# Opening of a two-block transformer kernel: modulation vectors and tokens taken tile by tile, gates and the first four weight jobs multiplied side by side

## The chip, the cores and the metric

The kernel runs on one core of one Trainium2 chip. The metric is the device time of one execution in microseconds (us). Three runs of the kernel before gave 2936.73 (the median), 2933.33 and 2941.17 us.

## What is computed

The reference is a stack of two blocks on 512 tokens of width 1024. Only the start of the first layer matters here: a modulation vector is computed from the condition `c`, the tokens are scaled and shifted by it, and the result `u` is multiplied by the input projection of an mLSTM mixer, whose columns are q, k, v, o and eight gate columns.

```
cs = jax.nn.silu(c)
for i in range(DEPTH):
    ada = cs @ w_ada[i] + b_ada[i]
    sh1, sc1, g1, sh2, sc2, g2 = [t[:, None, :] for t in jnp.split(ada, 6, axis=-1)]
    u = x * (1.0 + sc1) + sh1
    y = _mlstm_mixer(u, m_w_in[j], ...)        # even layers
# in _mlstm_mixer
proj = u @ w_in
qk, v, o, gates = jnp.split(proj, [s1, s2, s3], axis=-1)
qk = jax.nn.silu(_causal_dwconv(qk, conv_w, conv_b))
ig, lf = gates[..., :H], jax.nn.log_sigmoid(gates[..., H:])
```

All the rest (mixers, layer norms, FFNs, the second network) follows and is not touched.

## The kernel before, in words

Data is held transposed: features on the 128 partitions, tokens along the free side. `XT` is the stream in 8 tiles (KT = 8) of 128 features x 512 tokens. A weight matrix is cut into jobs of 128 output columns; a job is 128 x 8 x 128 numbers, 512 KB. There are 392 jobs (`wst`), numbered j in the order of the phases: `qk` (jobs 0 to 15), `v` (16 to 23), `gate_o` (24 to 31), `res` and so on.

Each job goes through the same line. SP loads it into one of two `RAW` slots (`load_raw`, L467; it waits for `lo_done` to reach j-1, so that the slot is free). ACT rounds it into `WH`, one of four slots (`round_hi`, L790, or `round_next`, L859; it waits for `pe_job` to reach j-3). POOL subtracts to get the low part `WL` (`lo`, L552). PE multiplies three times for each of 8 tiles: WH with the high part `U1h` of the input, WH with its low part `U1l`, WL with `U1h`, which is 24 matmuls of 128 x 512 (L1507). In `qk` DVE then applies a four-tap convolution (L1711, L1713) and ACT a SiLU (L949). In `v` ACT copies the result out (L953), PE turns it by four transposes (L1428), and DVE copies it into `VX` (L1809). The banks of `qk` and `v` are 0, 1, 4 and 7.

The modulation vectors are computed on DVE: a tile of `ast` (128 rows x 1024, 512 KB) is multiplied with `CB`, the SiLU of the condition, and summed along the row (`ada_sum`, L1637); four sums are then added to their bias and written to `MOD` (`ada_out`, L1649).

The opening of the kernel before has these steps:

- SP issues, in one queue: CB, 16 tiles of `ast` with their first slots in `ADA0` (8 slots), between them `PRM` (parameters), `GW` (gate weights), the whole `XT` behind tile 7, and the first two jobs behind tiles 10 and 12; then four constants, then the jobs from 2 on.
- DVE sums the 16 tiles, and only then writes `G2` = 1 + scale (L1686) and `B2` = shift (L1687) for all 8 tiles.
- ACT makes `U1h` and the full-precision copy `UF` tile by tile (L872, L873); DVE subtracts to get `U1l` (L1675).
- PE multiplies the gate weights with each tile as it comes (L1417, 24 matmuls into bank 2), and then jobs 0, 1, 2, ... one after the other.
- DVE works out the gate rows behind that (from L1693 to L1706), with an exponential and a logarithm from ACT (L878, L879). PE transposes the rows at the start of `v` (L1572).

Every engine executes its own instructions strictly in the order in which they are written; the order across engines is kept by semaphores.

Of the kernel before, what the change touches and what calls it, by code (L numbers as in the profile page):

```python
# [21 lines left out]
F32 = mybir.dt.float32  # L22
# [183 lines left out]
def build(nc, a, out):  # L206
    with ExitStack() as stack:
# [253 lines left out]
        def _(sp):  # L461
# [28 lines left out]
            for n, p in enumerate(phases):  # L490
                def body(i, p=p, ada_before=None):
                    for u in range(4):
                        if not (p["j0"] == 0 and is_first(i) and u < 2):
                            load_raw(i * 4 + (p["j0"] + u), u % 2)
# [288 lines left out]
        def _(act):  # L783
# [65 lines left out]
            def round_next(i, p, u):  # L849

                c = p["j0"] + u + 3
                if isinstance(i, int):
                    j = 4 * i + c
                    if j < njobs:
                        round_hi(j, j % 4)
                    return
# [20 lines left out]
            act.wait_ge(S("gate_abs"), 1)  # L877
            steps.link(act.activation(GR[0:4, 2], GR[0:4, 1], ACT.Exp))  # L878
            act.activation(GR[0:4, 3], GR[0:4, 2], ACT.Ln, bias=1.0).then_inc(S("gate_ln"), 1)  # L879
# [150 lines left out]
            for n, p in enumerate(phases):  # L1030
# [25 lines left out]
                if first(p, "v", 0):  # L1056
                    act.wait_ge(S("silu_done"), 16)
                if first(p, "res", 0):
# [352 lines left out]
        def _(pe):  # L1411

            pe.wait_ge(S("gate_lo"), 1)
            for k in range(KT):
                pe.wait_ge(S("u_ready"), k + 1)
                for m, (w, x) in enumerate(((GWh, U1h), (GWh, U1l), (GWl, U1h))):
                    mm = pe.matmul(BANK[2][:], w[:, k], x[:, k, 0:T], start=k == 0 and m == 0, stop=k == KT - 1 and m == 2)  # L1417
            mm.then_inc(S("gates_pe"), 1)
# [146 lines left out]
            for n, p in enumerate(phases):  # L1565
                if first(p, "v", 0):
                    pe.wait_ge(S("const_land"), 16 * 4)

# [21 lines left out]
                if first(p, "res", 1):  # L1590
# [26 lines left out]
        def _(dve):  # L1617
# [54 lines left out]
            def u_lo():  # L1672
                for t in range(KT):
                    dve.wait_ge(S("uf_done"), t + 1)
                    dve.tensor_tensor(U1l[:, t], UF[:, t, 0:T], U1h[:, t].bitcast(F32), ALU.subtract).then_inc(S("u_ready"), 1)  # L1675

            dve.wait_ge(S("prm_land"), 16)
            dve.wait_ge(S("cb_ready"), 1)
            for g in range(4):
                for u in range(4):  # L1680
                    j = 4 * g + u
                    dve.wait_ge(S(f"ada_begin{j % 8}"), 16 * (j // 8 + 1))
                    ada_sum(g, 0, u, ADA0[:, j % 8])
                ada_out(g, 0)
            dve.wait_ge(S("ada_evac"), 4)
            link(dve.tensor_scalar(G2[:, :, 0:1], mod(0, 1), 1.0, None, ALU.add))  # L1686
            dve.tensor_copy(B2[:, :, 0:1], mod(0, 0)).then_inc(S("g2_done"), 1)  # L1687
            u_lo()


            dve.wait_ge(S("gates_pe"), 1)
            gb = COL["gate_b"][0]
            link(dve.tensor_scalar(GR[0:4, 0], BANK[2][0:4, :], PRM[0:4, gb:gb + 1], None, ALU.add))  # L1693
            link(dve.tensor_scalar(GR[0:4, 5], BANK[2][32:36, :], PRM[32:36, gb:gb + 1], None, ALU.add))
            dve.scalar_tensor_tensor(out=GR[0:4, 1], in0=GR[0:4, 5], scalar=-1.0, in1=GR[0:4, 5], op0=ALU.mult, op1=ALU.min)\
                .then_inc(S("gate_abs"), 1)
            link(dve.tensor_scalar(GR[0:4, 4], GR[0:4, 5], 0.0, None, ALU.min))
            dve.wait_ge(S("gate_ln"), 1)
            link(dve.tensor_tensor(GR[0:4, 6], GR[0:4, 4], GR[0:4, 3], ALU.subtract))

            link(dve.tensor_tensor_scan(GR[0:4, 7], GR[0:4, 6], GR[0:4, 6], 0.0, ALU.add, ALU.bypass))
            link(dve.tensor_tensor(GM[0:4, 1], GR[0:4, 0], GR[0:4, 7], ALU.subtract))
            link(dve.tensor_tensor_scan(GM[0:4, 0], GM[0:4, 1], GM[0:4, 1], 0.0, ALU.max, ALU.bypass))
            dve.tensor_tensor(GM[0:4, 2], GR[0:4, 7], GM[0:4, 0], ALU.add).then_inc(S("gate_rows"), 1)
            dve.wait_ge(S("gate_rows"), 1)
            link(dve.memset(VX[:, :, :, DK:DK + 2], 1.0))  # L1706
# [498 lines left out]
            for n, p in enumerate(phases):  # L2205
# [5 lines left out]
                if first(p, "v", 0):  # L2211
                    dve.wait_ge(S("gate_cols_pe"), 1)
                    dve.tensor_copy(COLS[:], BANK[2][:, 0:32]).then_inc(S("gate_cols"), 1)
# [205 lines left out]
```

## Time and profile before

| | |
|---|---|
| median of the three runs | 2936.73 us |
| the profiled execution | 2937.88 us |
| its span, first to last instruction | 2936.1 us |
| granted TensorE clock, mean | 0.979 |
| PE busy | 2797.1 us, 95% of the span |
| DVE, POOL, ACT busy | 1593.2, 1093.2, 1046.6 us |
| moved from HBM | 324.50 MB, 111 GB/s over the span |

The page has, besides, the span in 40 slices of 73.4 us, the chain of work that ended last, and groups of instructions. A row of the timeline reads: start, time taken, engine, line, operation, output<-inputs, and in brackets how long its engine was idle before it and what ended that. PE is TensorE's matmuls, PEld its weight loads, SPq the queue of SyncE.

### The profile page before, as it was taken

How to read it: one execution, taken by the hardware profiler on the slowest of the kernel's cores; microseconds unless marked ns; L12 is line 12 of the kernel's file. 1: busy time of each engine (PE TensorE's matmuls, PEld its weight loads, DVE VectorE, ACT ScalarE, POOL GpSimd, SP SyncE). 2: the span in 40 equal slices, each digit the busy share in tenths (PEclk: the TensorE clock that was granted, in tenths of full speed). 3: DMA queues.
4: the chain of work that ended last, by engine and by line, in shares of the span. 5: the costliest groups of instructions: out<-in, count | busy, mean ns of one | idle time of the engine just before them, and what ended most of it. 6: DMA issues, size and time to landing. Idle time of an engine off the chain costs nothing.

```text
span 2936.1 us, 37960 instructions
## 1 busy us (share of the span) xinstructions
PE 2797.1 (95%) x13936; PEld 2391.5 (81%) x13936; DVE 1593.2 (54%) x2341; ACT 1046.6 (36%) x1689; POOL 1093.2 (37%) x510
## 2 busy tenths in 40 slices
PE   4998899999899899999999999999999999999998
PEld 3885788887776678887897999999997977778887
DVE  6536766966555669986522423755553487332111
ACT  3333353423465443324311232222223338443222
POOL 2440254444422254445531333323335233334443
PEclk9999899999999899999899999999999999999999
DMA  5351345553321145554111122333332122122232
GB/s 214 112 186 44 108 139 197 186 189 126 131 84 61 51 141 193 188 186 136 44 61 56 50 87 79 129 129 129 116 128 79 58 90 66 62 86 93 97 97 86
DMA packets 89955, 329.83 MB, mean 112 GB/s; under 512 B 9956, under 2 KB 10724, under 8 KB 89320
## 3 DMA queue, kind: packets, MB, share of 16 engines
q1 hardware_dynamic: 85392, 312.21, 30.6%
q10 hardware_dynamic: 4440, 16.00, 1.6%
q8 instruction: 75, 1.23, 0.2%
q14 instruction: 48, 0.39, 0.0%
HBM read 324.50 MB, written 2.10 MB: 111 GB/s over the span
## 4 chain that ended last, share of the span: by engine, by line
PE 58%; DVE 2%; POOL 1%; ACT 1%; issue 1%; DVEq 0%; ACTq 0%; POOLq 0%
PE pair L1505 26%; PE pair L1507 18%; PE bank L1507 4%; PE pair L1347 1%; PE bank L1300 1%; PE pair L1363 1%; PE bank L1380 1%; PE bank L1347 1%; PE bank L1437 0%; PE pair L1461 0%; PE pair L1320 0%; PE bank L1320 0%; POOL UF L534 0%; PE bank L1287 0%; POOL UF L538 0%
## 5 line engine op out<-in xcount | busy, mean ns | idle before, releaser
L552 POOL TENSOR_TENSOR WL<-RAW,WH 128x1024 fp32r<-128x1024 f32 x392 | 983.4, 2510 | 1679.0 <-ACT WH L859 1065.3
L859 ACT ACTIVATE WH<-RAW 128x1024 fp32r<-128x1024 f32 x276 | 290.3, 1052 | 351.3 <-PE pair L1505 181.5
L1637 DVE CUSTOM_DVE_ANT_0 ADA<-ADA,CB 128x1024 f32<-128x1024 f32 x128 | 237.7, 1863 | 117.2 <-DMA ADA<-in_ast 105.9
L1770 DVE SCALAR_TENSOR_TENSOR XT<-pair,GATE,XT 128x512 f32 (+1 forms) x96 | 72.0, 750 | 348.0 <-PE pair L1507 179.7
L1505 PE MATMUL pair<-Uh,WH 128*128 128x384 f32 x832 | 214.0, 338 | 2.1 <-issue 2.1
L1505 PE MATMUL pair<-Ul,WH 128*128 128x384 f32 x832 | 211.1, 334 | 0.0
L1505 PE MATMUL pair<-Uh,WL 128*128 128x384 f32 x832 | 211.1, 334 | 0.0
L1507 PE MATMUL bank<-U1h,WH 128*128 128x512 f32 x480 | 187.2, 390 | 0.0
L1507 PE MATMUL bank<-U1h,WL 128*128 128x512 f32 x480 | 186.8, 389 | 0.0
L1507 PE MATMUL bank<-U1l,WH 128*128 128x512 f32 x480 | 186.8, 389 | 0.0
L1507 PE MATMUL pair<-U1h,WH 128*128 128x512 f32 x448 | 175.5, 392 | 2.8 <-POOL WL L552 2.8
L1507 PE MATMUL pair<-Hh,WH 128*128 128x512 f32 x432 | 169.2, 392 | 8.1 <-DVE Hl L644 8.1
L1507 PE MATMUL pair<-U1h,WL 128*128 128x512 f32 x448 | 175.1, 391 | 0.0
L1507 PE MATMUL pair<-U1l,WH 128*128 128x512 f32 x448 | 174.9, 390 | 0.0
L1507 PE MATMUL pair<-Hl,WH 128*128 128x512 f32 x432 | 168.2, 389 | 0.0
L1507 PE MATMUL pair<-Hh,WL 128*128 128x512 f32 x432 | 168.1, 389 | 0.0
L790 ACT ACTIVATE WH<-RAW 128x1024 fp32r<-128x1024 f32 x116 | 122.1, 1053 | 105.9 <-DMA RAW<-in_wst 51.9
L1505 PEld LDWEIGHTS pair<-Uh,WH 128*128 128x128 f32 x832 | 150.3, 188 | 6.1 <-issue 6.0
L1505 PEld LDWEIGHTS pair<-Ul,WH 128*128 128x128 f32 x832 | 150.3, 188 | 0.0
L1505 PEld LDWEIGHTS pair<-Uh,WL 128*128 128x128 f32 x832 | 150.2, 188 | 0.0
L1826 DVE SCALAR_TENSOR_TENSOR TT<-pair,TT 128x512 f32<-128x512 f32 x64 | 44.3, 692 | 192.1 <-ACT TT L982 102.8
L1505 PE MATMUL pair<-Hh,WL 128*128 128x384 f32 x512 | 129.9, 334 | 0.0
(416 smaller groups left out, 6170.7 us busy)
## 6 DMA issues: line engine op xcount, KB each, us to landing
RAW<-in_wst SPq DMA_DIRECT2D x392, 512.0 KB, 3.5
ADA<-in_ast SPq DMA_DIRECT2D x192, 512.0 KB, 4.5
NB<-in_nbias ACTq DMA_DIRECT2D x8, 768.0 KB, 4.2
XT<-in_xt SPq DMA_DIRECT2D x1, 2048.0 KB, 15.4
STRIP<-in_strip ACTq DMA_DIRECT2D x8, 256.0 KB, 2.7
CB<-in_cb ACTq DMA_DIRECT2D x4, 512.0 KB, 4.1
DX<-in_dx ACTq DMA_DIRECT2D x1, 2048.0 KB, 8.0
out_xt<-XT SPq DMA_DIRECT2D x1, 2048.0 KB, 6.2
```

The source lines that it names most:

```text
L552: pool.tensor_tensor(WL[:, s4], RAW[:, s2], WH[:, s4].bitcast(F32), ALU.subtract)\
L790: act.activation(WH[:, u], RAW[:, u % 2], ACT.Copy).then_inc(S("hi_done"), 1)
L859: act.activation(WH[:, c % 4], RAW[:, c % 2], ACT.Copy).then_inc(S("hi_done"), 1)
L1300: mm = pe.matmul(BANK[bank][:, 0:w], FG[:, tok0 + i_, t, q * P:(q + 1) * P], mats[:, q, i_], start=i_ == 0 and q == 0, stop=i_ == tiles - ...
L1347: mm = pe.matmul(BANK[b][:], x[:, k, tok], flat(w[:, i, 4 * kk:4 * kk + 4]), start=k == 0 and m == 0, stop=k == KT - 1 and m == 2)
L1363: mm = pe.transpose(BANK[2 + c][:, s * P:(s + 1) * P], ZP[:, i % 3, c, s * P:(s + 1) * P], IDENT[:])
L1380: mm = pe.matmul(BANK[4][64 * c:64 * c + 64, b * P:(b + 1) * P], VN[:, tile, (2 * t + c) * NHD:(2 * t + c + 1) * NHD], PTN[:, i % 2, c, s ...
L1505: mm = pe.matmul(dst, w[:, u, k], x[:, k, c:c + HALF_TC], start=st and m == 0, stop=en and m == 2)
L1507: mm = pe.matmul(bank_of(p, u)[:], w[:, u, k], x[:, k, 0:T], start=st and m == 0, stop=en and m == 2)
L1637: dve.tensor_tensor_reduce(tile, tile, cb[:, 0], 1.0, 0.0, ALU.mult, ALU.add, AD[:, u, 0:1])\
L1770: ins = dve.scalar_tensor_tensor(out=flat(XT[:, ds(jl, 1)]), in0=bank[:], scalar=gate_of(jl), in1=flat(XT[:, ds(jl, 1)]), op0=ALU.mult, op ...
L1826: ins = dve.scalar_tensor_tensor(out=TT[:, u % 2, 0:T], in0=bank[:], scalar=0.0, in1=TT[:, u % 2, 0:T], op0=ALU.max, op1=ALU.mult)
```

## The change

- SP's order is by feature tile. For each k of 0 to 7 it loads the two `ast` tiles that this feature tile needs (row tile k, the shift, and row tile 8 + k, the scale) and then the 256 KB of `XT[:, k]`. Behind tile 0 come PRM, GW and jobs 0 and 1; behind tile 2 comes job 2, behind tile 3 job 3, each with its wait for `lo_done`. The wait of `XT[:, k]` is folded into the semaphore of the second `ast` tile.
- DVE, per k: two sums, the subtraction for tile k - 1 (`opening_lo`), and then `B2` and `G2` of tile k alone, which read the sums and the bias directly.
- ACT makes `U1h` and `UF` of tile t as soon as `g2_done` reaches t + 1. It rounds job 2 behind tile 2, job 3 behind tile 3, and jobs 4 and 5 behind tile 7. `round_next` then leaves out the jobs that have been rounded, and rounds job 6 between the first and second SiLU.
- PE (`opening`), per k: jobs 0 and 1 with tile k, the gates with tile k, and, from k = 2 on, jobs 2 and 3 with tile k - 2; the last two tiles of jobs 2 and 3 come at the end. Job 2's and job 3's first matmuls wait for `lo_done` of 3 and 4. These are the same 120 matmuls as before. The loop over `qk` then starts with job 4.
- The gate rows (DVE and ACT) move from behind the opening to the start of `v`, and their transposes on PE and the copy on DVE from the start of `v` to the start of `gate_o`.

```
-            for j in range(16):
-                at_least(sp, S("ada_done"), j - 7)
-                sp.dma_start(ADA0[:, j % 8], a["ast"][j]).then_inc(S(f"ada_begin{j % 8}"), 16)
-                if j == 1:
-                    sp.dma_start(PRM[:], a["prm"]).then_inc(S("prm_land"), 16)
-                if j == 3:
-                    sp.dma_start(GW[:], a["gw"]).then_inc(S("gw_land"), 16)
-                if j == 7:
-                    sp.dma_start(XT[:], a["xt"]).then_inc(S("x_land"), 16)
-                if j in (10, 12):
-                    load_raw(j // 2 - 5, j // 2 - 5)
+            for k in range(KT):
+                for n, j in ((2 * k, k), (2 * k + 1, KT + k)):
+                    at_least(sp, S("ada_done"), n - 7)
+                    sp.dma_start(ADA0[:, n % 8], a["ast"][j]).then_inc(S(f"ada_begin{n % 8}"), 16)
+                sp.dma_start(XT[:, k], a["xt"][:, k]).then_inc(S(f"ada_begin{(2 * k + 1) % 8}"), 16)
+                if k == 0:
+                    sp.dma_start(PRM[:], a["prm"]).then_inc(S("prm_land"), 16)
+                    sp.dma_start(GW[:], a["gw"]).then_inc(S("gw_land"), 16)
+                    load_raw(0, 0)
+                    load_raw(1, 1)
+                if k in (2, 3):
+                    load_raw(k, k % 2)
...
-            act.wait_ge(S("x_land"), 16)
-            act.wait_ge(S("g2_done"), 1)
             for t in range(KT):
+                act.wait_ge(S(f"ada_begin{(2 * t + 1) % 8}"), 32 * (t // 4 + 1))
+                act.wait_ge(S("g2_done"), t + 1)
                 act.activation(U1h[:, t], XT[:, t], ACT.Identity, ...)
                 act.activation(UF[:, t, 0:T], XT[:, t], ACT.Identity, ...)
-            round_hi(2, 2)
+                if t in (2, 3):
+                    round_hi(t, t)
+            round_hi(4, 0)
+            round_hi(5, 1)
...
+                for k in range(KT):
+                    pe.wait_ge(S("u_ready"), k + 1)
+                    for u in range(2):
+                        job(u, k)
+                    gates(k)
+                    if k >= 2:
+                        for u in range(2, 4):
+                            job(u, k - 2)
+                for u in range(2, 4):
+                    for k in range(KT - 2, KT):
+                        job(u, k)
...
+            for k in range(KT):
+                at_least(dve, S("g2_done"), k - 1)
+                for q in range(2):
+                    n = 2 * k + q
+                    dve.wait_ge(S(f"ada_begin{n % 8}"), (16 + 16 * q) * (n // 8 + 1))
+                    dve.tensor_tensor_reduce(ADA0[:, n % 8], ADA0[:, n % 8], CB[:, 0], 1.0, 0.0, ALU.mult, ALU.add,
+                                             AD[:, n % 4, 0:1]).then_inc(S("ada_done"), 1)
+                if k >= 1:
+                    opening_lo(k - 1)
+                dve.wait_ge(S("ada_done"), 2 * k + 2)
+                q = 2 * (k % 2)
+                dve.tensor_tensor(B2[:, k, 0:1], AD[:, q, 0:1], prm("bada", 2 * k), ALU.add)
+                dve.scalar_tensor_tensor(out=G2[:, k, 0:1], in0=AD[:, q + 1, 0:1], scalar=1.0, in1=prm("bada", 2 * (KT + k)),
+                                         op0=ALU.add, op1=ALU.add).then_inc(S("g2_done"), 1)
+            dve.wait_ge(S("g2_done"), KT)
+            dve.sem_inc(S("ada_evac"), 4)
+            opening_lo(KT - 1)
...
                 if first(p, "v", 0):
+                    gate_rows_dve()
+                if first(p, "gate_o", 0):
                     dve.wait_ge(S("gate_cols_pe"), 1)
```

## Rows read from the trace of the kernel before

**Rows 1.** The page: busy time, then two rows of its 40 slices.
```profile
PE 2797.1 (95%) x13936; PEld 2391.5 (81%) x13936; DVE 1593.2 (54%) x2341; ACT 1046.6 (36%) x1689; POOL 1093.2 (37%) x510
...
PE   4998899999899899999999999999999999999998
```
**Rows 2.** Timeline: PE at the opening, gates (L1417), then jobs 0 to 4 (L1507).
```profile
41.44 0.77 PE L1417 MATMUL pair<-U1h,GWh 128*128 128x512 f32 x1 [41.44 <-DVE U1l L1675]
42.01 0.63 PE L1417 MATMUL pair<-U1l,GWh 128*128 128x512 f32 x1
...
42.43 0.63 PE L1417 MATMUL pair<-U1h,GWl 128*128 128x512 f32 x1
...
47.42 0.40 PE L1417 MATMUL pair<-U1l,GWh 128*128 128x512 f32 x1
...
52.03 0.39 PE L1507 MATMUL pair<-U1h,WH 128*128 128x512 f32 x1
...
73.80 0.39 PE L1507 MATMUL pair<-U1h,WH 128*128 128x512 f32 x1
```
**Rows 3.** DMA issues in 0:80: count, size, median us to landing.
```profile
ADA<-in_ast SPq DMA_DIRECT2D x16, 512.0 KB, 11.9
...
PRM<-in_prm SPq DMA_DIRECT2D x1, 472.5 KB, 5.9
```
**Rows 4.** Timeline: the queue's first issue, then instructions that a landing released.
```profile
0.76 0.39 SPq L462 DMA_DIRECT2D CB<-in_cb  x1
...
4.33 1.06 ACT L862 ACTIVATE CB<-CB 128x1024 f32<-128x1024 f32 x1 [2.29 <-DMA CB<-in_cb]
...
8.03 1.23 DVE L1637 CUSTOM_DVE_ANT_0 ADA<-ADA,CB 128x1024 f32<-128x1024 f32 x1 [8.03 <-DMA PRM<-in_prm]
...
26.64 1.06 ACT L790 ACTIVATE WH<-RAW 128x1024 fp32r<-128x1024 f32 x1 [13.83 <-DMA RAW<-in_wst]
```
**Rows 5.** Timeline: POOL and DVE at 12, POOL at 144, DVE at 431.
```profile
12.89 2.34 POOL L556 TENSOR_TENSOR GWl<-GW,GWh 128x1024 fp32r<-128x1024 f32 x1 [12.42 <-ACT GWh L864]
13.04 3.26 DVE L1637 CUSTOM_DVE_ANT_0 ADA<-ADA,CB 128x1024 f32<-128x1024 f32 x1
...
144.90 5.74 POOL L552 TENSOR_TENSOR WL<-RAW,WH 128x1024 fp32r<-128x1024 f32 x2 [3.24 <-ACT WH L790]
...
431.00 2.36 DVE L1649 TENSOR_TENSOR MOD<-AD,PRM 128x4 f32<-128x4 f32 x1
```
**Rows 6.** Timeline: small DVE work, ACT's pair and DVE's subtraction for one tile.
```profile
38.78 0.17 DVE L1687 COPY B<-MOD 128x8 f32<-128x8 f32 x1
39.05 0.81 ACT L872 ACTIVATE U1h<-XT,B,G 128x512 fp32r<-128x512 f32 x1 [7.65 <-DVE B L1687]
39.77 0.80 ACT L873 ACTIVATE UF<-XT,B,G 128x512 f32<-128x512 f32 x1
...
40.60 0.69 DVE L1675 TENSOR_TENSOR U1l<-UF,U1h 128x512 fp32r<-128x512 f32 x1 [1.65 <-ACT UF L873]
```
**Rows 7.** Windows late in the kernel; columns end in granted clock, DMA share, GB/s.
```profile
2218.00:2222.00 4.00, 2.78 (x9) 2.13 (x9) 3.88 (x5) 1.67 (x3) 1.64 (x2) 0.50 0.00 0
```
**Rows 8.** Timeline of PE in that stretch.
```profile
2220.16 0.77 PE L1461 MATMUL pair<-Uh,WH 128*128 128x512 f32 x1 [1.22 <-ACT Uh L913]
...
2225.19 0.39 PE L1461 MATMUL pair<-Uh,WH 128*128 128x512 f32 x1
```
**Rows 9.** Timeline: gate rows now, first and last DVE step, and ACT's logarithm.
```profile
52.23 0.74 DVE L1693 TENSOR_SCALAR GR<-pair,PRM 4x512 f32<-4x512 f32 x1 [1.06 <-PE pair L1417]
...
56.44 0.63 ACT L879 ACTIVATE GR<-GR 4x512 f32<-4x512 f32 x1
...
63.87 0.09 DVE L1706 MEMSET VX<- 128x32 f32 x1
```
**Rows 10.** Timeline: the start of `v` on ACT and PE.
```profile
143.05 0.63 ACT L949 ACTIVATE QK<-TT 128x512 f32 x1 [3.85 <-DVE TT L1713]
...
150.78 0.60 PE L1428 MATMUL bank<-IDENT,TT 128*128 128x128 f32 x4
```

More of the change, by code:

```diff
@@ L492, in body @@
                     for u in range(4):
-                        if not (p["j0"] == 0 and is_first(i) and u < 2):
+                        if not (p["j0"] == 0 and is_first(i)):
                             load_raw(i * 4 + (p["j0"] + u), u % 2)
@@ L853, in round_next @@
                     j = 4 * i + c
+                    if c == u + 3 and i == 0:
+                        j = 6 if u == 1 else njobs
                     if j < njobs:
@@ L874, in _, with gate_rows_act @@
                     .then_inc(S("uf_done"), 1)
-            round_hi(2, 2)
-            act.wait_ge(S("gate_abs"), 1)
-            steps.link(act.activation(GR[0:4, 2], GR[0:4, 1], ACT.Exp))
-            act.activation(GR[0:4, 3], GR[0:4, 2], ACT.Ln, bias=1.0).then_inc(S("gate_ln"), 1)
+                if t in (2, 3):
+                    round_hi(t, t)
+            round_hi(4, 0)
+            round_hi(5, 1)
+            def gate_rows_act():
+                act.wait_ge(S("gate_abs"), 1)
+                steps.link(act.activation(GR[0:4, 2], GR[0:4, 1], ACT.Exp))
+                act.activation(GR[0:4, 3], GR[0:4, 2], ACT.Ln, bias=1.0).then_inc(S("gate_ln"), 1)
             def ln_act(p, idx):
@@ L1411, in _, with opening, gates, job @@
         def _(pe):
[L1413 to L1418, printed above, removed]
+            def opening():
+                def gates(k):
+                    if k == 0:
+                        pe.wait_ge(S("gate_lo"), 1)
+                    for m, (w, x) in enumerate(((GWh, U1h), (GWh, U1l), (GWl, U1h))):
+                        mm = pe.matmul(BANK[2][:], w[:, k], x[:, k, 0:T], start=k == 0 and m == 0, stop=k == KT - 1 and m == 2)
+                    if k == KT - 1:
+                        mm.then_inc(S("gates_pe"), 1)
+                def job(u, k):
+                    if k == 0:
+                        pe.wait_ge(S("lo_done"), u + 1)
+                    for m, (w, x) in enumerate(((WH, U1h), (WH, U1l), (WL, U1h))):
+                        mm = pe.matmul(bank_of(phases[0], u)[:], w[:, u, k], x[:, k], start=k == 0 and m == 0,
+                                       stop=k == KT - 1 and m == 2)
+                    if k == KT - 1:
+                        mm.then_inc(S("pe_job"), 1)
+                for k in range(KT):
[9 more added lines that the diff above has]
+                        job(u, k)
+            opening()
             def v_turn(i, p, u):
@@ L1589, in _ @@
                     neighbourhood_pe(pe)
-                if first(p, "res", 1):
+                if p["j0"] == 0:
+                    rounds(pe, p["n"] // 4 - 1, lambda i, p=p: stream(i + 1, p))
+                elif first(p, "res", 1):
                     stream(1, p)
@@ L1670, in rms_gains @@
                 link(dve.tensor_copy(B2[:, :, 0:n], mod(layer, vec, 0, n)))
[L1672 to L1675, printed above, removed]
             dve.wait_ge(S("prm_land"), 16)
             dve.wait_ge(S("cb_ready"), 1)
[L1679 to L1706, printed above, removed]
+            def opening_lo(t):
+                dve.wait_ge(S("uf_done"), t + 1)
+                dve.tensor_tensor(U1l[:, t], UF[:, t, 0:T], U1h[:, t].bitcast(F32), ALU.subtract).then_inc(S("u_ready"), 1)
@@ L2211, in _ @@
                 if first(p, "v", 0):
+                    gate_rows_dve()
+                if first(p, "gate_o", 0):
                     dve.wait_ge(S("gate_cols_pe"), 1)
```

17 lines of the change are left out of this document (added).

## Prediction

> **What bounds the kernel now.** I read the page first: PE is busy 95% of the span and near full in nearly every slice but the first [rows 1]. So a microsecond is won only where PE idles or is late, and the first slice is such a place. The timeline of PE there shows it idle until 41.44, then the gates, waiting for each tile, and jobs from 52.03 on, with nothing between them; job 4 starts at 73.80 [rows 2]. That instant is the whole measure of this change: from job 4 on the work is as before, so whatever job 4 gains, the end gains, unless a later stall takes it back. PE owes 120 matmuls before job 4 (24 for the gates, 96 for jobs 0 to 3). Their pitch is (73.80 - 52.03) / 96 = 0.227 us at full clock, 27.2 us in all, and 0.42 us in the first gates [rows 2]. So PE is given its tiles too late, and the question is when they can come.
>
> **The queue.** All bytes go through SP's one queue and land in order: CB (0.52 MB) is used at 4.33, PRM as the fourth transfer (2.06 MB in total) at 8.03, job 0 (9.92 MB) at 26.64 [rows 3, 4]. That is a rate of 0.42 MB/us, so a transfer is usable at 4.33 + (MB before its end - 0.52) / 0.42. The bytes don't change, only the order. By the new order: tile 0 at 7.5, PRM 8.6, GW 9.9, job 0 11.1, job 1 12.4, tile 1 15.5, tile 2 18.6, job 2 19.9, tile 3 23.0, job 3 24.2, then a tile each 3.1 us to tile 7 at 36.7. New: SP waits ahead of job 2 for the first `lo`, with the tiles 3 to 7 queued behind it. CB took 3.6 us from issue to use [rows 4], and the wait ends at 15.9 (below), so job 2 still comes by 19.9 and the wait costs nothing; its cover ends if `lo` is later than 16.3.
>
> **DVE and POOL.** This is what I think now sets the pace. A sum takes 1.22 us, but 3.26 when a POOL subtraction of 2.34 has begun just before; two POOL subtractions around a sum took 5.74 together; even a 128x4 addition took 2.36 once, where such small steps take 0.17 [rows 5, 6]. So an instruction with two inputs in SBUF and a POOL subtraction take turns, whole instruction by whole instruction. The Trainium skill says the same (SBUF — State Buffer, "Who interferes with whom": an exclusive lock), and the trace agrees by the 2.36 us row.
>
> Per tile DVE has two sums (2.3 us start to start), one subtraction (0.69) and two small ones (0.17 each) [rows 4, 6]: 3.35 us, slightly more than the 3.1 us of the queue. POOL's GWl and four `lo` add 5 turns of 2.4. Taking turns from 8.7: DVE sums tile 0 till 11.1; GWl 11.05 to 13.4; `lo` of job 0 till 15.9; of job 1 till 18.4, with B2 and G2 of tile 0 between. Sums and B2/G2 of tile 1 till 21.7, of tile 2 till 25.05. `U1l` of tile 0 is there at 21.4. ACT needs 1.5 us per tile [rows 6] and then rounds job 2 till 27.65; `lo` of job 2 gets its turn 28.1 to 30.5. G2 of tile 3 waits for it, is there at 30.8, ACT makes tile 3 till 32.4 and only then rounds job 3, till 33.4; its `lo` waits for two sums and a subtraction and ends at 36.25. From there DVE needs 3.35 us a tile: G2 of tile 7 at 46.65, the last `U1l` at 49.0 (38.78 and about 51 now).
>
> **PE.** It takes tiles 0, 1 and 2 between 21.4 and 30.8, then stands at job 3's first matmul until 36.3, because jobs 2 and 3 are taken up at k = 2. By then 30 of 120 matmuls are done. The other 90 take 20.4 us at 0.227, and each of their tiles is there in time. To this I add the clock. The first 13 gates ran at a pitch of 0.42, the lower of the two levels (1.2 GHz), and by 47.42 they had the upper one; late in the kernel, behind stops of PE, the granted clock is 0.50 and PE needs from 2220.16 to 2225.19 before a matmul of that shape takes 0.39 again [rows 2, 7, 8]. A stop of 5.5 us stands before the 90 matmuls, so I charge 13 of them the difference, 13 x 0.19 = 2.5. The bounds are 0 (the clock stays) and 5 (it comes back late). Job 4 thus starts at 36.3 + 20.4 + 2.5 = 59.2, and the gain is 73.8 - 59.2 = 14.6 us.
>
> A rule of the Trainium skill bears on this term: TensorE: Matmul & The Clock Gate, "What's actually happening", has the slow clock as the default and activity as what lifts it. By the rule the restart is slow and the sum is 14.6; if the stretch before the stop still counted, it would be 17.1. The rows at 2220 agree with the rule.
>
> **What goes elsewhere.** Job 4 must be rounded and subtracted between the end of job 0 and its start. Behind job 0's last matmul there are 24 others, 5.45 us; rounding and `lo` take 1.06 + 2.4 + 0.2 = 3.7. So 1.7 us are spare, and without them the price is what is missing. The four convolutions come in one burst on DVE and job 7 is rounded only behind them; it is not wanted before jobs 4 to 6 are through, 16 us: free.
>
> The gate rows at the start of `v` put a wait into ACT, with the rounding of job 19 and the copy of job 16 queued behind it, and fill DVE for 63.87 - 52.23 = 11.6 us, with its sum for the next vector and VX behind. Now the logarithm ends 4.85 us after DVE's first step [rows 9]. DVE is free at 142.9, just ahead of the last SiLU [rows 10]; so ACT is free at 147.8, rounds job 19 till 148.8 and copies job 16 till 149.4. PE's transposes of it come at 150.78 [rows 10], 1.4 us to spare; job 19 is wanted 6 us after them (24 matmuls and four transposes), also free. DVE, with two turns lost to POOL, reaches VX of job 16 at about 161; PE wants that two jobs behind 150.78, near 163. Both are close, so I charge 0, with 0 to 3 as bounds. The moved transposes and copy cost 0.7 wherever they stand. PE's, SP's and ACT's counts of instructions stay; DVE saves four small ones.
>
> **The sum.** Against the profiled execution: 2937.9 - 14.6 = 2923.3. The median of the runs is 1.15 below that execution, so 2922.2.
>
> **The rivals.** (A) One turn better: if G2 of tile 3 gets ahead of `lo` of job 2, all that follows is 2.2 us earlier, `lo` of job 3 ends at 34.05, and job 4 starts at 57.0, or at 54.5 if the clock also holds. The next bound is then the last `U1l`, 46.8 + 27 matmuls x 0.227 = 52.9. Gains of 17 to 19, 2917.5 to 2920. For it: turns hang on tenths of a microsecond. (B) Small waits add up: the 1.7 and 1.4 us of slack are used up, `v` stalls by 2 or 3 us, a `lo` comes one turn (2.4) later. Gain 5 to 10, 2927 to 2932. (C) No change: the clock stays low through the whole opening, as PE works in short bursts. 90 matmuls at 0.42 end at 74.1, so job 4 is no earlier and the time is 2937. The Trainium skill describes such a pattern (TensorE: Matmul & The Clock Gate, "HAM oscillation — how this bites in real kernels"). Against it: behind 36.3 PE has all its data and runs without a stop, as from 41.44, where the clock rose after 5.6 us [rows 2]. (D) Slower: the chain of turns is worse than I have it, so that job 4 comes behind 73.8. It needs SP held up: job 2, and behind it tile 3 and job 3, hang on `lo` of job 0. Were that at 31 instead of 15.9 (as now, where job 0 lands at 26.64), job 2 would land at 34.6 and job 3 at 39; with the 12 us that I have from job 3's landing to the end of its `lo` (24.2 to 36.25), and 22.9 of PE behind it, job 4 starts at 73.9. That is the point from which it decides; each us beyond costs one, and at 33 the time is 2939. Against it: 3.4 MB are ahead of the end of job 0 instead of 9.9. (E) The order doesn't matter since the bytes are the same: the last tile lands at 36.7, where by the same rate the last `ast` tile landed at 34.2 before (13.07 MB), and the tiles are ready at 49 instead of 51. True of the tiles, but the gain is in the 96 matmuls that lay behind them, so I give it nothing of its own.
>
> **How the numbers follow.** Forecast as summed, gains of 10 to 17: 0.55. A: 0.15. B: 0.20. C: 0.06. D: 0.04. The measurement tells about 0.3% of the kernel, 8.8 us, from no change. Faster by more than that: the forecast, A and a third of B, 0.76; within: the rest of B and C, 0.19; slower 0.05. The range is 2916 to 2931.5: it holds the forecast, A with both clock bounds and the scatter of a median of three runs below it, and most of B, and leaves out C, D and the worst of B.
>
> **What would show it.** PE's first matmul near 21.4 instead of 41.44; sums of 3.3 us where POOL works; a stop of PE for `lo` of job 3 until about 36; a pitch of 0.42 behind it for some 5 us; job 4 near 59; in `v` no idle PE ahead of the transposes. The forecast is wrong if PE waits for `u_ready` between tiles 3 and 7, if SP stands behind 16.3, or if the time saved by job 4 is not there at the start of `gate_o`.

## The result and the profile after

The changed kernel took 2918.53 us (median of 4 runs, 2916.05 to 2919.61) beside 2937.74 us for the kernel before (4 runs): a ratio of 0.9939, 95% interval 0.9927 to 0.9951. That is 19.2 us faster, where 14.6 us were forecast. Measured twice more (below) the gain was 15.5 and 13.9 us.

| | after |
|---|---|
| the profiled execution, its span | 2918.07, 2916.3 us |
| granted TensorE clock, mean | 0.977 |
| PE busy | 2795.3 us, 96% of the span |

The page shows the gain in one digit, that of the first slice, which was 4 [rows 1]. The work of PE is the same 13936 matmuls.

```profile
PE 2795.3 (96%) x13936; PEld 2390.7 (82%) x13936; DVE 1601.9 (55%) x2351; ACT 1045.7 (36%) x1688; POOL 1097.7 (38%) x510
...
PE   6998899999999899999999999999999999999998
```

The timeline of PE at the opening of the changed kernel, against [rows 2]: start, time taken, engine, line, operation.

```profile
21.81 0.79 PE L1436 MATMUL pair<-U1h,WH 128*128 128x512 f32 x1 [21.81 <-DVE U1l L1714]
22.40 0.63 PE L1436 MATMUL pair<-U1l,WH 128*128 128x512 f32 x1
...
31.27 0.39 PE L1436 MATMUL bank<-U1h,WL 128*128 128x512 f32 x1
...
35.32 0.80 PE L1436 MATMUL bank<-U1h,WH 128*128 128x512 f32 x1 [3.65 <-POOL WL L553]
35.91 0.63 PE L1436 MATMUL bank<-U1l,WH 128*128 128x512 f32 x1
...
41.03 0.55 PE L1436 MATMUL bank<-U1l,WH 128*128 128x512 f32 x1
41.41 0.39 PE L1436 MATMUL bank<-U1h,WL 128*128 128x512 f32 x1
...
58.64 0.39 PE L1542 MATMUL pair<-U1h,WH 128*128 128x512 f32 x1
```

The reader is to see four instants: the first matmul at 21.8 (41.44 before), the stop ahead of job 3 until 35.3, the slow matmuls behind it until 41.4, and job 4 at 58.64 (73.80 before). So 15.16 us are won at job 4: PE begins 19.6 us earlier and gives back 3.65 in the stop and the rest in the slow matmuls. The other 4.6 of the 19.8 us between the two spans must come later.

DVE and POOL, against [rows 4 to 6]:

```profile
9.77 1.23 DVE L1721 CUSTOM_DVE_ANT_0 ADA<-ADA,CB 128x1024 f32<-128x1024 f32 x1 [9.77 <-DMA PRM<-in_prm]
...
12.12 2.35 POOL L557 TENSOR_TENSOR GWl<-GW,GWh 128x1024 fp32r<-128x1024 f32 x1 [11.66 <-ACT GWh L867]
12.19 2.31 DVE L1727 TENSOR_TENSOR B<-AD,PRM 128x1 f32<-128x1 f32 x1
...
27.57 2.52 POOL L553 TENSOR_TENSOR WL<-RAW,WH 128x1024 fp32r<-128x1024 f32 x1 [7.51 <-ACT WH L791]
27.75 2.35 DVE L1727 TENSOR_TENSOR B<-AD,PRM 128x1 f32<-128x1 f32 x1
30.03 0.15 DVE L1728 SCALAR_TENSOR_TENSOR G<-AD,PRM 128x1 f32<-128x1 f32 x1
...
32.81 2.45 POOL L553 TENSOR_TENSOR WL<-RAW,WH 128x1024 fp32r<-128x1024 f32 x1 [2.73 <-ACT WH L791]
32.99 2.29 DVE L1727 TENSOR_TENSOR B<-AD,PRM 128x1 f32<-128x1 f32 x1
...
46.10 0.69 DVE L1714 TENSOR_TENSOR U1l<-UF,U1h 128x512 fp32r<-128x512 f32 x1 [1.65 <-ACT UF L876]
```

Three additions of 128 numbers, B2 of tiles 0, 3 and 4, last 2.3 us instead of 0.15, each as long as the POOL subtraction that began just ahead of it. These are the turns of the prediction.

The waits of PE behind the opening, up to 240 us, show what `v` took back (columns: who waited for whom, us in total, times, longest):

```profile
PE bank L1164 <- DMA SEL<-in_sel: 3.5, 1, 3.5
PE bank L1152 <- DVE HN L2086: 0.8, 1, 0.8
PE bank L1463 <- ACT TT L961: 0.6, 2, 0.4
```

The wait for SEL was there before (3.4 us), that for HN was not. The transposes at L1463 wait twice for ACT's copy, 0.6 us together against 0.3 once before. Followed over the matmuls of the jobs alone, the lead is 15.2 at job 4, 15.8 at the start of `v` (the eight gate transposes no longer stand there), 15.4 behind the first copy of ACT (the late copy costs 0.5) and 14.6 in `gate_o`, where the transposes now stand (0.8). So `v` and the moved transposes keep 0.6 us of the 15.2.

### The profile page after: what moved, and what is told of

It reads as the page before. It is cut to its first block, busy times and chain, and to the rows that moved or that the text cites. A ratio compares the mean times of both kernels' runs of the same rounds, so it can differ in the third digit from the quotient of the medians.

```text
span 2916.3 us, 37982 instructions
## 1 busy us (share of the span) xinstructions
PE 2795.3 (96%) x13936; PEld 2390.7 (82%) x13936; DVE 1601.9 (55%) x2351; ACT 1045.7 (36%) x1688; POOL 1097.7 (38%) x510
## 4 chain that ended last, share of the span: by engine, by line
PE 58%; DVE 2%; POOL 1%; issue 1%; ACT 1%; DVEq 0%; ACTq 0%; POOLq 0%
PE pair L1540 26%; PE pair L1542 18%; PE bank L1542 4%; PE pair L1356 1%; PE bank L1309 1%; PE pair L1372 1%; PE bank L1389 1%; PE bank L1356 1%; PE bank L1472 0%; PE pair L1496 0%; PE pair L1329 0%; PE bank L1329 0%; POOL UF L535 0%; PE bank L1296 0%; POOL UF L539 0%
## 5 line engine op out<-in xcount | busy, mean ns | idle before, releaser
L1674 DVE CUSTOM_DVE_ANT_0 ADA<-ADA,CB 128x1024 f32<-128x1024 f32 x112 | 213.4, 1906 | 106.1 <-DMA ADA<-in_ast 103.3
L1542 PE MATMUL bank<-U1h,WH 128*128 128x512 f32 x464 | 180.9, 390 | 0.0
L1542 PE MATMUL bank<-U1h,WL 128*128 128x512 f32 x464 | 180.6, 389 | 0.0
L1542 PE MATMUL bank<-U1l,WH 128*128 128x512 f32 x464 | 180.5, 389 | 0.0
L1542 PE MATMUL pair<-U1h,WH 128*128 128x512 f32 x432 | 168.5, 390 | 2.6 <-POOL WL L553 2.6
L1542 PE MATMUL pair<-U1h,WL 128*128 128x512 f32 x432 | 168.1, 389 | 0.0
L1542 PE MATMUL pair<-U1l,WH 128*128 128x512 f32 x432 | 168.1, 389 | 0.0
```

What stands on the lines that cost most here:

```text
L1542: mm = pe.matmul(bank_of(p, u)[:], w[:, u, k], x[:, k, 0:T], start=st and m == 0, stop=en and m == 2)
L1674: dve.tensor_tensor_reduce(tile, tile, cb[:, 0], 1.0, 0.0, ALU.mult, ALU.add, AD[:, u, 0:1])\
```

## Where the other 4.6 us came from

Matmul by matmul, the lead stays near 15 us up to 725 us and then grows in three steps, to 17.0 near 740, 18.6 near 1046 and 19.8 near 1393. At each step the same matmuls run at the low clock before and at the high clock after. The windows of the second step (columns: stretch, its length, busy time of the five engines, then granted clock, DMA share, GB/s), first the kernel before, then the changed kernel:

```profile
1044.00:1047.00 3.00, 3.00 (x9) 2.32 (x8) 1.30 (x1) 1.05 (x2) 0.76 (x1) 0.50 0.77 262
```
```profile
1024.00:1028.00 4.00, 2.32 (x10) 1.98 (x11) 3.56 (x3) 1.45 (x2) 3.79 (x2) 1.00 0.32 106
```

Both stand behind the same stop of PE for a POOL subtraction (2.79 us before, 2.60 after). Before, the matmuls turn slow 1.2 us after the restart, and eight of them start 0.40 to 0.43 us apart; after, none does. Nothing that the change touches runs there. Is that chance of one execution, or a lasting effect of having everything earlier? Four runs were for this.

**The changed kernel again.** The kernel is unchanged.

> The changed kernel once more, as it is, with more rounds and a second profile. In the first profiles job 4 starts 15.2 us earlier than before, v gives back 0.7 and gate_o starts 14.5 to 15.0 us early, yet the end is 19.8 us early: the other 4.7 us appear in three stretches where matmuls run at the low clock (near 730, 1045 and 1393 us). Theory 1: where the stretches of low clock fall is chance of the single execution, so the gain over many rounds is 14.5 to 15.5 us and in a second profile the lead at the end differs from 19.8 by more than 1 us. Rival: it is a lasting gain; the rounds give 18 to 20 us and the second profile shows steps of lead at the same places.

Measured: 2921.58 us (5 runs) beside 2937.08 (23 runs), ratio 0.9947, interval 0.9934 to 0.9960, a gain of 15.5 us. In its profile job 4 starts at 58.80, and the leads over the first profile of before are 15.0 at job 4, 14.4 in `gate_o`, 15.1 at 300 us, then 16.1 (345 us), 17.9 (1046), 15.5 to 17.3 (around 1400) and 17.0 at the last matmul. The time of the five runs and the lead at the end are as theory 1 has them, and the step near 740 is gone. But the step near 1046 is there again, 1.6 us as in the first profile, as the rival has it. The windows behind that stop of PE, in the second profile of before (next run) and in this one:

```profile
1046.00:1049.00 3.00, 3.00 (x9) 2.32 (x8) 1.41 (x1) 0.88 (x1) 0.86 (x1) 0.53 0.64 239
```
```profile
1025.00:1029.00 4.00, 2.72 (x12) 2.27 (x13) 3.93 (x1) 0.00 (x0) 3.39 (x2) 1.00 0.46 133
```

The same stop can be read in all 14 profiles of this document. No slow matmul stands behind it in the eight of the changed kernel and of its variants that start job 4 by 58.8 us (stops of 1.98 to 2.78 us); seven or eight stand behind it in the five of before (twice), serial, two and rows_early (2.77 to 2.84 us); none in shift (1.92 us). So this step is no chance of one execution: some 1.6 us of the later lead recur with the changed kernel. Whether the length of the stop or the instant decides is open, since both differ between the two groups.

**The kernel before again.** No edit.

> The kernel before, once more, for its profile. Theory 1 (chance): the total of the stretches with low granted clock, or the places where they begin and end against the work, differ from the first profile, and PE's instants late in the kernel differ by 1 to 4 us although those before 230 us agree within 0.2. Rival (lasting): both profiles of before agree within 0.5 us at every matmul.

Measured: 2939.54 us in the one run. Until 236 us its PE instants stand 0.8 us behind those of the first profile, which is the later first tile, then up to 0.8 us ahead of them until 729, 2.1 us behind by 937, and 1.6 us behind at the last matmul, with stretches of low clock at 936.9 and 971.1 that are not in the first profile (that has one at 965.4). So two executions of one kernel drift apart by about 2 us with no edit between them. I had expected 0.2 us before 230 us; the difference of 0.8 shows that the arrival of the data varies too.

**A shift of everything.** One line more in the kernel before:

```
             sp.dma_start(CB[:, 0], a["cb"][0]).then_inc(S("cb_land"), 16)
+            sp.wait_ge(S("cb_land"), 16)
```

> The kernel before, with the whole program delayed at its start: SP waits for its first transfer (CB, usable at 4.33 us) before it issues the next. Everything behind comes about 3.3 to 3.6 us later and nothing else changes. Theory 1: the time grows by just that, 3 to 4 us over many rounds. Rival (stretches of low clock keep a fixed phase against the start of the program, so that a shift changes their overlap with the work): the time changes by less than 1 or more than 6 us.

Measured: 2940.06 us (12 runs, 2934.49 to 2946.03) beside 2937.08, ratio 1.0010, interval 1.0001 to 1.0018: 3.0 us, at least 0.3 and at most 5.3. In its profile PRM is used at 10.28 instead of 8.03 and job 4 comes 2.25 us later, not the 3.3 to 3.6 I had said. Part of what the wait adds must lie beside a latency that was there anyway; that is argued, no row splits it. A shift of 2.25 us appears in the time as about that, within a wide interval, and the first tile of two executions of before itself came 0.8 us apart.

**And a third time**, beside late_fill (below):

> The changed kernel once more, beside late_fill on one chip. Theory 1: 15 us below the kernel before, as in the second measurement (15.5), and within 1.5 us of 2921.6; rival: the first measurement (19.2) was the typical one.

Measured: 2923.0 us (5 runs, 2919.21 to 2925.0) beside 2936.91, ratio 0.9948, interval 0.9934 to 0.9961, a gain of 13.9 us; job 4 at 58.74. Weighted by the runs, the three measurements give (4 x 19.2 + 5 x 15.5 + 5 x 13.9) / 14 = 16.0 us. The lead at job 4 over the first profile of before was 15.16, 15.00 and 15.06, the lead at the last matmul 19.8, 17.0 and 14.9. So the excess of the first measurement is within what executions of one kernel differ by, and the profiles show through what: where the low clock falls behind PE's stops. One of its steps, that near 1046, is in all three profiles (1.6 us each time), so it is not scatter; the one near 1393 (1.2 us) is in the first and the third. Whether the lasting gain is the 14.6 us of `gate_o` or 1 to 2 us more, the times can't tell. What decides where the low clock falls, no run here shows.

## The experiments on the opening

**The parts of the gain.** First, the tile order alone, with PE's old order:

```
                 for k in range(KT):
                     pe.wait_ge(S("u_ready"), k + 1)
-                    for u in range(2):
-                        job(u, k)
                     gates(k)
-                    if k >= 2:
-                        for u in range(2, 4):
-                            job(u, k - 2)
-                for u in range(2, 4):
-                    for k in range(KT - 2, KT):
+                for u in range(4):
+                    for k in range(KT):
                         job(u, k)
```

> One part alone: data arrive tile by tile as in the change, but PE multiplies only the gates with each tile, and jobs 0 to 3 one after the other behind them, as before. Read is the start of job 4 (58.6 changed, 73.8 before). Theory 1 (nearly all of the gain is the 96 matmuls that were moved under the arrival; the earlier last tile is worth its own 4.4 us): the last U1l is ready at 46.8, the gates end near 47.8, 96 matmuls take 21.8, job 4 starts at 69.5, or at 72 if the clock is still low when they begin. Rival (the tile order brings the gain and the order on PE little): job 4 below 64.

Measured: job 4 at 72.18, and 2939.2 us in one run. The timeline of PE, at its last tile:

```profile
45.56 0.63 PE L1428 MATMUL pair<-U1h,GWl 128*128 128x512 f32 x1
47.02 0.80 PE L1428 MATMUL pair<-U1h,GWh 128*128 128x512 f32 x1 [0.83 <-DVE U1l L1709]
...
51.88 0.63 PE L1436 MATMUL pair<-U1h,WL 128*128 128x512 f32 x1
52.30 0.54 PE L1436 MATMUL pair<-U1h,WH 128*128 128x512 f32 x1
52.68 0.40 PE L1436 MATMUL pair<-U1l,WH 128*128 128x512 f32 x1
```

and in the kernel before, at its last tile:

```profile
51.22 0.50 PE L1417 MATMUL pair<-U1h,GWh 128*128 128x512 f32 x1 [0.45 <-DVE U1l L1675]
```

This is the 72 of theory 1. PE was busy with three matmuls in every 3.0 to 5.2 us, and they stayed slow until 52.3, although the last tile was there at 47.0. So the last tile comes 4.2 us earlier (47.02 beside 51.22), and job 4 only 1.6: 2.6 are lost, to the low clock for the most part. Without PE's new order the new order of the data is worth 1.6 of the 15.2 us at job 4, and the one run is no faster than the kernel before (2936.13).

That does not make the other 13.6 the worth of PE's order alone. That half was not run by itself, but the rows of before bound it: PE can't begin ahead of its first tile, at 41.44, and 120 matmuls (27.2 us) with 13 of them at the low clock (2.5) end at 71.1, so PE's order with the old order of the data could win 2.7 us at most. This is an estimate from [rows 2]. Neither half is worth 3 us, both together 15.2: the first tile at 21.8 makes the room, and PE's order fills it. This run is also where rival C was real: in it the bursts of three matmuls a tile stayed slow to the end, while in the next one, with nine a tile, the matmuls became fast.

**Jobs 2 and 3 side by side or not.**

```
                     gates(k)
-                    if k >= 2:
-                        for u in range(2, 4):
-                            job(u, k - 2)
                 for u in range(2, 4):
-                    for k in range(KT - 2, KT):
+                    for k in range(KT):
                         job(u, k)
```

> Jobs 0 and 1 side by side with the gates as tiles arrive, jobs 2 and 3 one after the other behind tile 7. PE then never waits for lo of job 3, but has 9 + 48 matmuls left behind the last U1l at 46.8. Theory 1: job 4 at 46.8 + 57 x 0.227 = 59.8 if the clock is high by then, up to 62 if it has stayed low in the short bursts (9 matmuls for every 3.0 us). So jobs 2 and 3 side by side are worth 1 to 3.5 us. Rival (their wait for lo of job 3 costs more than they bring): job 4 earlier than 58.4.

Measured: job 4 at 60.22, with five waits for `U1l` (27.6 us in all, 22.1 of them the first) and none for `lo`; 2927.55 us in one run. As theory 1 has it, at its high-clock end. Taking up jobs 2 and 3 early is worth 60.22 - 58.64 = 1.6 us at job 4 (0.3 of it is the later first tile of this execution), no more, since their stop for `lo` and the clock behind it eat the rest. The time lies 6 us above the changed kernel's 2921.6, which is more; it is one run, and in its profile the further loss stands where matmuls are slow, near 772 and 937 us and at the stop near 1046.

**The stop and the clock.** Fifteen matmuls into a free bank, whose result nobody reads, fill the stop:

```
                 def job(u, k):
                     if k == 0:
+                        if u == 3:
+                            fill(15)
                         pe.wait_ge(S("lo_done"), u + 1)
```

> The changed kernel with 15 extra matmuls (gate weights x tile 0 into an unused bank, result not used) in the stop of PE ahead of job 3's first matmul. They take 15 x 0.227 = 3.4 us of a stop of 3.65, so the work behind is not later, but PE is busy through it. In the changed kernel 13 of the next 90 matmuls run at 0.42. Theory 1 (the clock term: these are slow because PE stood still): no matmul at 0.42 behind 35.3, job 4 at 35.3 + 20.4 + 0.2 = 55.9 instead of 58.6 to 58.8. Rival (the low stretch has its own timing, whatever PE does): 12 or 13 slow matmuls stay, job 4 at 58.6.

Measured: job 4 at 56.33, 2920.17 us in one run. The timeline of PE around the stop:

```profile
31.38 3.56 PE L1434 MATMUL pair<-U1h,GWh 128*128 128x512 f32 x15
35.80 0.50 PE L1442 MATMUL bank<-U1h,WH 128*128 128x512 f32 x1 [0.85 <-POOL WL L553]
36.13 0.40 PE L1442 MATMUL bank<-U1l,WH 128*128 128x512 f32 x1
36.37 0.39 PE L1442 MATMUL bank<-U1h,WL 128*128 128x512 f32 x1
```

and the windows of 36 to 44 us, of this kernel and of the changed one (granted clock third from the end):

```profile
36.00:44.00 8.00, 8.00 (x36) 6.61 (x36) 8.00 (x17) 4.49 (x6) 0.00 (x0) 1.00 0.71 272
```
```profile
36.00:44.00 8.00, 8.00 (x26) 6.36 (x25) 8.00 (x19) 4.01 (x6) 0.00 (x0) 0.67 0.67 259
```

No matmul at 0.42 is left behind the stop. `lo` came 0.48 us later in this execution, so the clock term is 58.64 + 0.48 - 56.33 = 2.8 us, of which 0.26 is the slower first matmul. It had been charged at 2.5, and it is shown to be the stop that costs it: this is one execution, but in each of the four profiles that have the stop unfilled (after, after_again, after_third and rows_early, 3.65 to 4.12 us) 11 to 14 slow matmuls follow it.

**Rounding job 3 earlier.**

```
-                if t in (2, 3):
-                    round_hi(t, t)
+                if t == 2:
+                    round_hi(2, 2)
+                    round_hi(3, 3)
```

> ACT rounds job 3 right behind job 2, ahead of tile 3. Theory 1 (turns between DVE and POOL): lo of job 3 ends at 32.7 instead of 35.3, but it takes its turn between B2 and G2 of tile 3, so that G2 comes at 32.7 instead of 30.0 and the U1l of tile 3 at 35.7 instead of 33.1; PE stands first for lo, then for that tile, and then has 87 matmuls: job 4 at 35.7 + 19.7 + 0 to 2.5 = 55.4 to 58.0, the last U1l at about 47.6. Rival (the wait for lo is all that counts): job 4 at 32.7 + 20.4 + 0 to 2.5 = 53.1 to 55.6, with no wait for U1l.

Measured: job 4 at 56.87, 2922.39 us in one run. The timeline of DVE, and of PE:

```profile
27.82 2.35 DVE L1728 TENSOR_TENSOR B<-AD,PRM 128x1 f32<-128x1 f32 x1
30.10 0.15 DVE L1729 SCALAR_TENSOR_TENSOR G<-AD,PRM 128x1 f32<-128x1 f32 x1
30.17 3.40 DVE L1722 CUSTOM_DVE_ANT_0 ADA<-ADA,CB 128x1024 f32<-128x1024 f32 x1
```
```profile
32.53 0.50 PE L1437 MATMUL bank<-U1h,WH 128*128 128x512 f32 x1 [1.35 <-POOL WL L553]
35.38 0.51 PE L1437 MATMUL pair<-U1h,WH 128*128 128x512 f32 x1 [1.89 <-DVE U1l L1715]
```

The instants at PE are as theory 1 gave them (32.7 and 35.7), but the order of turns is not: G2 follows B2 at once, and it is the sum behind G2 that waits (3.40 instead of 1.21) until POOL is through. The waiting POOL subtraction did not get in between these two short DVE instructions. Either way a turn that POOL takes earlier is one that DVE takes later: `lo` is 2.8 us earlier, the `U1l` of tile 3 2.3 us later, and job 4 1.8 us earlier, with eight slow matmuls behind the two stops.

**Jobs 2 and 3 one tile later**, which turns the wait for `lo` into one for a tile:

```
-                    if k >= 2:
+                    if k >= 3:
                         for u in range(2, 4):
-                            job(u, k - 2)
+                            job(u, k - 3)
                 for u in range(2, 4):
-                    for k in range(KT - 2, KT):
+                    for k in range(KT - 3, KT):
```

> Jobs 2 and 3 are taken up at k = 3 instead of k = 2 (three tiles behind, so that their last three tiles stand at the end); nothing else. PE then stands for U1l of tile 3 (ready at 33.1) instead of for lo of job 3 (35.3), and has 93 matmuls behind that. Theory 1: job 4 at 33.1 + 21.1 = 54.2 if the clock stays high over the shorter stop, 56.8 if it falls; the limit behind the last U1l, 46.8 + 33 x 0.227 = 54.3, is the same. The time falls by 1.8 to 4.3 us against the changed kernel (2921.6), to 2917.3 to 2919.8, which beats both kernels. Rival (the gain is lost behind, in the rounding of job 4 or in the convolutions): job 4 early, time within 1 us of the changed kernel.

Measured: job 4 at 56.17, 2920.54 us (5 runs) beside 2936.13, ratio 0.9947, interval 0.9933 to 0.9960: a gain of 15.6 us. The stop is 2.57 us (until 33.15) and eight matmuls behind it are slow. So job 4 is 2.5 us earlier, near the 56.8 said for a clock that falls, but the time forecast from it (2917.3 to 2919.8) was missed: 1 us below the changed kernel's 2921.6, on another chip, is no measurable difference, and neither theory is told from the other.

**Both: later jobs and a filled stop** (11 extra matmuls ahead of tile 3):

> Both: jobs 2 and 3 three tiles behind (job 4 at 56.2, with 8 slow matmuls behind the stop) and 11 extra matmuls in the stop ahead of tile 3 (30.4 to 33.15). Theory 1: job 4 at 33.15 + 93 x 0.227 + 0.2 = 54.5, 4.2 us ahead of the changed kernel; 0.5 to 1 us of it is lost at the start of v, so the time is 3 to 4 us below the changed kernel beside it. Rival (a few us at job 4 don't reach the end, as late_jobs, 2.6 us ahead at job 4, came out only 1 us below the changed kernel): within 1.5 us of the changed kernel.

Measured: job 4 at 56.99, 2921.15 us (5 runs) beside 2936.91 and beside the changed kernel's 2923.0; ratio to the kernel before 0.9948, interval 0.9934 to 0.9961. The fill did keep the clock, and then the next thing was late:

```profile
39.15 0.50 PE L1440 MATMUL pair<-U1h,WH 128*128 128x512 f32 x1 [1.40 <-DVE U1l L1720]
```

My 54.5 had left out that the `U1l` of tile 4 is held up by `lo` of job 3 (B2 of tile 4 takes 2.35 us in this profile). Behind it stand 78 matmuls, 17.7 us, which gives 56.9. The data were 0.8 us late in this execution. So with this order the bound is the turn, whether the clock holds or not. The time is 1.9 us below the changed kernel beside it, between the 3 to 4 us of theory 1 and the 1.5 us of its rival, and within the scatter of either.

**Sums to PSUM.** The same turns, tried from DVE's side:

```
-                                             AD[:, n % 4, 0:1]).then_inc(S("ada_done"), 1)
+                                             BANK[3][:, n % 4:n % 4 + 1]).then_inc(S("ada_done"), 1)
...
-                dve.tensor_tensor(B2[:, k, 0:1], AD[:, q, 0:1], prm("bada", 2 * k), ALU.add)
-                dve.scalar_tensor_tensor(out=G2[:, k, 0:1], in0=AD[:, q + 1, 0:1], scalar=1.0, ...
+                dve.tensor_tensor(B2[:, k, 0:1], BANK[3][:, q:q + 1], prm("bada", 2 * k), ALU.add)
+                dve.scalar_tensor_tensor(out=G2[:, k, 0:1], in0=BANK[3][:, q + 1:q + 2], scalar=1.0, ...
```

> The changed kernel with one thing moved: the row sums of the opening are written to PSUM instead of SBUF, so that B2 and G2 have one input in SBUF and one in PSUM; nothing is left out. In the changed kernel B2 of tiles 0, 3 and 4 took 2.3 us each beside a POOL subtraction instead of 0.15. Theory 1 (only an instruction with two inputs in SBUF takes turns with POOL): all B2 take about 0.2 us, also beside a POOL subtraction; G2 of tile 3 comes at 27.9 instead of 30.0, ACT is through with rounding job 3 at 30.6 instead of 32.7, lo of job 3 ends near 33.7 instead of 35.3; but then a sum loses the turn, so U1l of tile 3 comes at about 35.4 instead of 33.1, and 87 matmuls stand behind it: job 4 at 55.2 to 57.7 instead of 58.7. The time is 1 to 3 us below the changed kernel (2921 to 2923), at the edge of what five rounds tell. Rival (any DVE instruction waits for POOL): B2 stays at 2.3 us and job 4 at 58.7.

Measured: job 4 at 55.46, 2921.84 us (5 runs, 2916.91 to 2927.71) beside 2936.06, ratio 0.9957, interval 0.9943 to 0.9971. The timeline of DVE at tile 3, where `lo` of job 2 runs from 27.96 to 30.53:

```profile
28.21 0.14 DVE L1727 TENSOR_TENSOR B<-pair,PRM 128x1 f32<-128x1 f32 x1
28.27 0.14 DVE L1728 SCALAR_TENSOR_TENSOR G<-pair,PRM 128x1 f32<-128x1 f32 x1
28.33 3.29 DVE L1721 CUSTOM_DVE_ANT_0 ADA<-ADA,CB 128x1024 f32<-128x1024 f32 x1
31.55 3.35 DVE L1721 CUSTOM_DVE_ANT_0 ADA<-ADA,CB 128x1024 f32<-128x1024 f32 x1
```

With one input in PSUM the additions run beside POOL in 0.14 us; the sum behind them, with both inputs in SBUF, waits. The rule of the Trainium skill (SBUF — State Buffer, "Who interferes with whom") names just these: a DVE instruction with two inputs in SBUF waits for a POOL one that reads SBUF, one with a single input there does not. This trace agrees on both sides of it, on one instruction: 2.35 and 0.14 us. `lo` of job 3 ended at 33.8 and the `U1l` of tile 3 at 35.6, as said (33.7, 35.4), and no slow matmul followed the stops of 2.32 and 0.77 us. At job 4 this is the best of all, 3.2 us ahead of the changed kernel, but in the time it can't be told from it.

**The gate rows back behind the opening.** DVE's and ACT's calls of the gate rows stand at their old place, the transposes at `gate_o`.

> The changed kernel with one part undone: the gate rows stay right behind the opening, on DVE and ACT, instead of at the start of v (their transposes stay at gate_o). DVE would start them when the gates end, near 53.7, and need 11.6 us, and only then convolve job 0 (3.1 us), so that bank 0 comes free at about 68.5 instead of 56.5, where job 4 wants it at 58.6. Theory 1: PE stands 9 to 10 us at job 4, v loses nothing, the gain shrinks from its value to about 6 us (0.7 us comes back in v). Rival: the move of the gate rows was not needed, since DVE catches up; then the time is within 2 us of the changed kernel.

Measured: 2934.67 us (10 runs) beside 2937.08, ratio 0.9989, interval 0.9980 to 0.9998. Against the changed kernel on the same chip that is 13.1 us lost.

```profile
55.15 0.74 DVE L1739 TENSOR_SCALAR GR<-pair,PRM 4x512 f32<-4x512 f32 x1 [7.97 <-PE pair L1429]
...
65.38 0.81 DVE L1759 TENSOR_SCALAR TT<-pair,PRM 128x512 f32<-128x512 f32 x1
```
```profile
68.60 0.80 PE L1543 MATMUL pair<-U1h,WH 128*128 128x512 f32 x1 [9.40 <-DVE TT L1761]
```

PE stands 9.4 us at job 4 for the bank of job 0, as computed, and then restarts on the low clock: the lag grows from 9.8 to 11.7 us within nine matmuls. That last term had been left out of the expectation, which said a gain of about 6 us. Another 1.4 us of the 13.1 are not accounted for by PE's instants up to there. Thus the least conspicuous part of the change carries most of it: without it, 2.4 of 15.5 us are left.

## Why the prediction was right, point by point

- **What bounds it.** Held: PE's work is untouched, and job 4's start (forecast 59.2, measured 58.64) is where the gain is made.
- **The queue.** The rate held, the start did not: PRM was usable at 9.77 instead of 8.6 and job 0 at 12.2 instead of 11.1. In the windows of 6 to 8 us, when the first 256 KB of `XT` pass, the rate is 251 and 271 GB/s, where it was 401 and 415 before:

```profile
6.00:7.00 1.00, 0.00 (x0) 0.00 (x0) 0.00 (x0) 0.00 (x0) 0.00 (x0) 1.00 0.97 251
7.00:8.00 1.00, 0.00 (x0) 0.00 (x0) 0.00 (x0) 0.00 (x0) 0.00 (x0) 1.00 0.93 271
```

  I had charged that tile by its bytes. It cost about 1.1 us more, and moved PE's first matmul by 0.4 and nothing at the end. SP's wait for the first `lo` ended at 16.8 instead of 15.9. That is past 16.3, which I had named as a sign of being wrong, but it cost nothing: job 2 was there when ACT came to it at 26.45, and no gap behind the wait reached DVE. That limit was put too tightly.
- **DVE and POOL.** The turns are the step that carried the forecast, and they came as worked out, with G2 of tile 3 at 30.0 (30.8) and `lo` of job 3 ending at 35.3 (36.25). The term of 3.35 us per tile was mis-sized: it is 3.03 (G2 of tiles 5 and 6 are at 38.24 and 41.27), since instructions overlap by 0.08 us each and B2 and G2 start 0.07 us apart. So the last `U1l` was there at 46.8 instead of 49.0. It did not bind.
- **PE.** First matmul 21.8 (21.4), stop until 35.3 (36.3), 90 matmuls behind it in 23.3 us (22.9). The stop was 3.65 us and not 5.5: besides the earlier `lo`, PE's first 30 matmuls ran without a wait, 13 of them at the low clock, which I had not charged there, and filled part of it. The clock term of 2.5 us behind the stop is confirmed by fill (2.8). That 58.64 came so near 59.2 is in part luck: DVE began 1.1 us later than I had it (9.77 for 8.7) and the clock term was 0.4 too small, while the turns from there to the end of `lo` of job 3 were 2 us shorter (25.5 for 27.55).
- **Elsewhere.** Job 4 did not wait. ACT's copy of job 16 was not free as charged: it ran from 134.73 for 0.57 us, and the transposes started at 135.35, 0.39 us late, of 0.6 us that PE waited there in all. I had named no idle PE ahead of the transposes as a sign of being right; there was some, and with it 14.6 of the 15.2 us reach `gate_o`. The moved transposes cost 0.8 us there where they had cost 0.7 at `v`, and the backlog of DVE was gone by 160 us. The counts of instructions were wrong, at no price: DVE has ten more (16 of B2 and G2 for two, less four of MOD) and SP seven more (`XT` in eight pieces).
- **The sum.** 14.6 forecast, 15.2 at job 4. The time of the first measurement was 3.7 us below the forecast, inside its range, by low clock elsewhere in the kernel, of which the prediction has nothing; the two later ones were 0.6 below and 0.8 above. Rival A would give the first number too, but for a wrong reason: there was no better turn in that profile. Rivals B, C (for this kernel) and D did not occur.
- **What could not be shown:** no variant beats the changed kernel in time. Five of them start job 4 by 1.6 to 3.2 us earlier, and the three of these that were run five times (2920.5, 2921.2 and 2921.8 us) lie among its own three medians, 2918.5, 2921.6 and 2923.0. Whether their lead is lost or hidden in the scatter stays open. PE's new order with the old order of the data was not run.

## What to carry to other kernels

When work waits for data that come in pieces, the first piece sooner and work to put under the arrival pay only together (1.6 us for the one, 2.7 at most for the other, 15.2 for both): put as many jobs as buffers allow under the arrival, and then look at what else the idle engines did in that gap, since it now needs a new place (here the gate rows, 13 of 15 us). Count the turns of DVE and POOL instruction by instruction, small ones too, and give one input to PSUM where a small one is in the way. And for an effect of half a per cent read the start of the next untouched stage in several profiles: it was the same to 0.2 us in three profiles of the changed kernel and to 0.8 in two of the kernel before, where the times of one kernel scattered by up to 12 us. Before calling a later step chance, look for it in the other profiles: one of three was in all of them.

## What the runs showed of the hardware that I had not expected

- Two executions of one kernel drift apart by 2 us or more over 2900 us (before and before_again 2 us from 937 us on, after and after_third 4.9 us at the end), by where the granted clock falls. A stop of 2.79 us had eight slow matmuls behind it, one of 2.60 us none, and one of 2.57 us, at another place, eight. At one stop, that near 1046, the outcome recurred: the same in all eight profiles with an early job 4, and the other in all five with a late one.
- An addition of 128 numbers takes 2.3 us beside a POOL subtraction, and 0.14 us with one of its inputs in PSUM.
- The first 256 KB slice, 2 KB from each 16 KB row, brought the queue from 401 and 415 to 251 and 271 GB/s for about 2 us (234 to 259 GB/s over these 2 us in four more profiles with this order, 399 in before_again). Later slices did much less: 356 GB/s at worst in 2 us, where the kernel before, without slices, has 383 at worst while its queue is full. Why the first is worse was not tried.
